# Order of weight loads and activation stores on the sync queue of a PEER decoder kernel

## The reference

```python
q = (xt @ w_q).reshape(T, 8, 2, 128)                   # queries, 8 heads, two halves
s = jnp.einsum('thpc,hpnc->thpn', q, sub_keys)
s1, i1 = lax.top_k(s[:, :, 0], 16)
s2, i2 = lax.top_k(s[:, :, 1], 16)
top_s, top_j = lax.top_k(cand, 16)                     # cand: the 16 x 16 sums of s1 and s2
expert = jnp.take_along_axis(cidx, top_j, axis=-1)     # 16 experts for each token and head
gate = jax.nn.softmax(top_s, axis=-1)
h = jax.nn.gelu(jnp.einsum('cd,chkd->chk', xc, u[ec])) # u, v: 16384 x 1024, f32
out = jnp.einsum('chk,chkd->cd', gc * h, v[ec])
```

## Time and profile before

| | us |
|---|---|
| median of 3 runs | 3217.59 (3217.42 to 3220.31) |
| the profiled execution, its own time | 3212.85 |
| its span | 3211.1 |
| PE busy in the span | 3122.8 (97%) |
| DVE busy | 2582.2 (80%) |
| ACT busy | 1630.2 (51%) |
| POOL busy | 1098.8 (34%) |

### The profile page before, as it was taken

How to read it: one execution, slowest core, us unless ns; L and a number is a source line. 1 busy time by engine, 2 the same in 40 slices (tenths; PEclk the granted TensorE clock), 3 DMA queues, 4 the chain that set the end, 5 groups by cost and what they waited for, 6 DMA issues and landing times. The chain is left out here.

```text
span 3211.1 us, 48802 instructions
## 1 busy us (share of the span) xinstructions
PE 3122.8 (97%) x17820; PEld 2787.3 (87%) x17820; DVE 2582.2 (80%) x5352; ACT 1630.2 (51%) x3075; POOL 1098.8 (34%) x658
## 2 busy tenths in 40 slices
PE   8999999999999999999999989999999999999999
PEld 7878899999998888888978868899999998888887
DVE  5686898989867888885368876898989866888885
ACT  5343249686853333334346654248686853333333
POOL 1002464646432444430000001365646432345440
PEclk9999999999999999999999999999999999999999
DMA  5113269998998999994222214259998998999994
GB/s 194 44 61 132 90 222 348 317 371 313 383 380 316 378 393 394 393 358 136 75 84 75 87 60 152 79 197 342 317 374 317 371 381 322 379 399 394 391 373 146
DMA packets 331165, 846.03 MB, mean 263 GB/s; under 512 B 27600, under 2 KB 160304, under 8 KB 323760
## 3 DMA queue, kind: packets, MB, share of 16 engines
q1 hardware_dynamic: 252592, 557.68, 48.3%
q0 software_dynamic: 78336, 285.25, 23.9%
HBM read 735.77 MB, written 107.05 MB: 262 GB/s over the span
## 5 line engine op out<-in xcount | busy, mean ns | idle before, releaser
L2545 ACT ACTIVATE peer_hi<-raw 128x1024 fp32r<-128x1024 f32 x540 | 570.9, 1057 | 706.3 <-PE p_bank L2476 623.1
L2888 DVE TENSOR_TENSOR peer_lo<-raw,peer_hi 128x1024 fp32r<-128x1024 f32 x434 | 530.6, 1223 | 303.3 <-ACT peer_hi L2545 285.2
L2358 POOL TENSOR_TENSOR peer_lo<-raw,peer_hi 128x1024 fp32r<-128x1024 f32 x106 | 272.7, 2574 | 1044.1 <-ACT peer_hi L2545 1043.7
L2376 POOL DMA_INDIRECT p_grow<-in_v_rows,p_expert x256 | 394.4, 1541 | 473.6 <-DVE p_acc L2912 381.8
L2376 POOL DMA_INDIRECT p_grow<-in_u_rows,p_expert x256 | 377.4, 1474 | 438.8 <-DVE p_hid L2903 388.7
L2476 PE MATMUL p_bank<-peer_hi,p_w_hi 128*128 128x512 f32 x1500 | 461.8, 389 | 0.0
L2476 PE MATMUL p_bank<-peer_hi,p_w_lo 128*128 128x512 f32 x1500 | 461.8, 389 | 0.0
L2476 PE MATMUL p_bank<-peer_lo,p_w_hi 128*128 128x512 f32 x1500 | 461.7, 389 | 0.0
L2402 PE MATMUL p1r_h_ps<-h_hi,peer_hi 128*128 128x368 f32 (+2 forms) x1152 | 393.7, 342 | 10.6 <-DVE peer_lo L2888 5.4
L2402 PE MATMUL p0r_h_ps<-h_hi,peer_hi 128*128 128x368 f32 (+2 forms) x1152 | 395.6, 343 | 7.7 <-DVE peer_lo L2888 5.3
L2402 PE MATMUL p0r_h_ps<-h_hi,peer_lo 128*128 128x368 f32 (+2 forms) x1152 | 389.3, 338 | 0.0
(11 more groups left out here) (481 smaller groups left out, 5615.3 us busy)
## 6 DMA issues: line engine op xcount, KB each, us to landing
raw<-in_u SPq DMA_DIRECT2D x256, 512.0 KB
raw<-in_v SPq DMA_DIRECT2D x256, 512.0 KB
p_g_sb<-gates SPq DMA_DIRECT2D x64, 768.0 KB
hiddens<-p_h_sb SPq DMA_DIRECT2D x240, 192.0 KB
p_w_raw<-hiddens SPq DMA_DIRECT2D x60, 768.0 KB
gates<-x SPq DMA_DIRECT2D x24, 1024.0 KB
raw<-in_w_b_mix SPq DMA_DIRECT2D x38, 512.0 KB, 3.5
raw<-in_w_peer_q SPq DMA_DIRECT2D x32, 512.0 KB, 4.3
```

The lines of the kernel that those rows point to most:

```text
L2358: pool.tensor_tensor(lo[:, m % NH, :], raw[:, m % NR, :], hi[:, m % NH, :].bitcast(F32), ALU.subtract).then_inc(lo_pool, 1)
L2376: pool.indirect_dma_start(out=grow[:, g % RG, :], out_offset=None, in_=table, in_offset=bass.IndirectOffsetOnAxis(ap=names[:, at:at + 1], ...
L2545: act.activation(hi[:, n % NH, :], raw[:, n % NR, :], ACT.Copy).then_inc(hi_ready, 1)
L2888: dve.tensor_tensor(lo[:, m % NH, :], raw[:, m % NR, :], hi[:, m % NH, :].bitcast(F32), ALU.subtract).then_inc(lo_dve, 1)
```

## The change

The load of block n+5 now stands ahead of the store of block n-1 in the sync list; before, it was the load of block n+4 behind that store. One load is put ahead of the loop for it. `h_sb` has four buffers instead of two. A group of gates is stored in four pieces of 512 KB, in steps s, s+1, s+2 and s+3, instead of two of 1 MB in s and s+1. To make room for the buffers, `xfew` lies in `qT` (its load moves from step 4 to step 18 and waits for the last scores) and `few_row` lies in `table`.

```diff
+    HB = 4
+    GATE_PARTS = 4
-        h_sb = st.sb("h_sb", [P, 2, SD])
+        h_sb = st.sb("h_sb", [P, HB, SD])
-            xfew = early.sb("xfew", [P, D])
+            xfew = qT[:, :, :].rearrange("p a b -> p (a b)")
-            few_row = early.sb("few_row", [P, HK])
+            few_row = table[:, BATCH * NK:BATCH * NK + HK]
             def store_g(b, part):
                 sp.wait_ge(g_moved, (b + 1) * (TB // GROUP))
-                at = slice(part * NK // 2, (part + 1) * NK // 2)
+                at = slice(part * NK // GATE_PARTS, (part + 1) * NK // GATE_PARTS)
...
             def load_few_x():
                 sp.wait_ge(few_x_stored, 16)
+                sp.wait_ge(scored, NQ)
...
+            load(NR)
             for n in range(BLOCKS + 1):
+                if n + 1 + NR < BLOCKS:
+                    load(n + 1 + NR)
                 if NQ < n <= FRONT - HELD * CH:
                     store_h(n - 1)
-                if n + NR < BLOCKS:
-                    load(n + NR)
                 if n == 2:
                     store_few_x()
-                if n == 4:
+                if n == NQ + 2:
                     load_few_x()
...
-                if n in store_at:
-                    store_g(store_at[n], 0)
-                if n - 1 in store_at:
-                    store_g(store_at[n - 1], 1)
+                for part in range(GATE_PARTS):
+                    if n - part in store_at:
+                        store_g(store_at[n - part], part)
...
-                if j >= 2:
-
-                    act.wait_ge(h_stored[j % 2], 16 * (j // 2))
+                if j >= HB:
+
+                    act.wait_ge(h_stored[j % HB], 16 * (j // HB))
...
-                    act.wait_ge(g_stored[b % 2], 32 * (b // 2))
+                    act.wait_ge(g_stored[b % 2], 16 * GATE_PARTS * (b // 2))
```

More of the change, by code:

```diff
@@ L2171, in peer_stage @@
         loaded = [st.sem(f"loaded{r}") for r in range(NR)]
-        h_stored = [st.sem(f"h_stored{r}") for r in range(2)]
+        h_stored = [st.sem(f"h_stored{r}") for r in range(HB)]
         g_stored = [st.sem(f"g_stored{r}") for r in range(2)]
@@ L2249, in store_h @@
                 sp.wait_ge(taken, n + 1)
-                sp.dma_start(h_dram[j // CH, :, j % CH, :], h_sb[:, j % 2, :]).then_inc(h_stored[j % 2], 16)
+                sp.dma_start(h_dram[j // CH, :, j % CH, :], h_sb[:, j % HB, :]).then_inc(h_stored[j % HB], 16)
             def store_g(b, part):
                 sp.wait_ge(g_moved, (b + 1) * (TB // GROUP))
-                at = slice(part * NK // 2, (part + 1) * NK // 2)
+                at = slice(part * NK // GATE_PARTS, (part + 1) * NK // GATE_PARTS)
                 sp.dma_start(g_dram[:, (b + 1) % NTD, at, :], gbuf[b % 2][:, at, :]).then_inc(g_stored[b % 2], 16)
@@ L2259, in load_hidden @@
                 at = chunk_source(c)
-                for r in range(2):
-                    sp.wait_ge(h_stored[r], 16 * (at + 1) * CH // 2)
+                for r in range(HB):
+                    sp.wait_ge(h_stored[r], 16 * (at + 1) * CH // HB)
                 sp.dma_start(w_raw[:, c % 2, :, :], h_dram[at]).then_inc(h_loaded[c % 2], 16)
@@ L2266, in load_gates @@
                     for r in range(2):
-                        sp.wait_ge(g_stored[r], 32 * (NTD // 2))
+                        sp.wait_ge(g_stored[r], 16 * GATE_PARTS * (NTD // 2))
                 else:
@@ L2281, in load_few_x @@
                 sp.wait_ge(few_x_stored, 16)
-                sp.dma_start(xfew[:, :], few_x_dram.rearrange("t q d -> (t q) d")).then_inc(few_x_loaded, 16)
+                sp.wait_ge(scored, NQ)
+                sp.dma_start(xfew, few_x_dram.rearrange("t q d -> (t q) d")).then_inc(few_x_loaded, 16)
             def store_few():
@@ L2561, in take @@
                     return
-                if j >= 2:
-                    act.wait_ge(h_stored[j % 2], 16 * (j // 2))
-                else:
-                    unit(h_sb[:, j % 2, 0:NE])
-                act.activation(h_sb[:, j % 2, NE:SD], h_ps[:, n % 2, P + NE:S], ACT.Gelu).then_inc(taken, 1)
+                if j >= HB:
+                    act.wait_ge(h_stored[j % HB], 16 * (j // HB))
+                else:
+                    unit(h_sb[:, j % HB, 0:NE])
+                act.activation(h_sb[:, j % HB, NE:SD], h_ps[:, n % 2, P + NE:S], ACT.Gelu).then_inc(taken, 1)
             def unit(to):
@@ L2898, in use_row @@
                         dve.wait_ge(few_x_loaded, 16)
-                    dve.tensor_tensor_reduce(row, row, xfew[:, :], 1.0, 0.0, ALU.mult, ALU.add,
+                    dve.tensor_tensor_reduce(row, row, xfew, 1.0, 0.0, ALU.mult, ALU.add,
                                              few_hid[:, at:at + 1]).then_inc(used, 1)
```

## The result

| | before | changed kernel |
|---|---|---|
| median, us | 3217.51 (3211.48 to 3220.31) | 3181.48 (3175.87 to 3183.22) |
| the profiled execution, its own time | 3212.85 | 3181.07 |
| span | 3211.1 | 3179.3 |

What follows compares the result with a forecast made beforehand. PE was taken to bound the kernel, with gaps caused by transfers by way of ACT. 20 us of gaps plus 4.4 of clock less 2.5 of added wait made 22 us, from 3217.6 to 3195.6 us; range 3180 to 3212.

Steps and rivals of the forecast that it cites:

- the forecast proper: Whole kernel: 12 to 32 us won, centred on 22 us or 3195.6 us; chance 0.58.
- What bounds it: PE, busy 97% of the span; only its gaps can be won, 30.7 us ended by ACT at the u blocks.
- The load's lead and the buffers: Sync queue: loads get 13 to 17 us instead of 8 to 10, activation stores 16 to 20.
- How much of the gaps goes: PE gaps ended by ACT at the u blocks: 65% goes, 20 of 30.7 us in both layers.
- Step 130: Behind the third stretch: the wait at `load_gates` grows to perhaps 10 us; only 30% of 4.05 us of gaps goes.
- Gate pieces: Gate stores: 1.25 MB a step instead of 1.77, leaving 4 us of backlog instead of 7.
- Their added wait: Gate buffer reuse: the last piece leaves two steps ahead of ACT's copy instead of four; 2.5 us lost.
- The clock: PE's lower clock level after gaps ended by ACT, 1.7 us lost in one window; 4.4 us won back.
- The gaps at the routing: PE gaps ended by DVE behind the routing, 5.4 us in one row: said to stay as they were.
- the sum 20 + 4.4 - 2.5: Whole kernel: gaps won, plus clock won, less the added gate buffer wait, gives 22 us.
- The signs: ACT's store waits near 0, u-block waits under 20 us; PE's column and copy gaps about 10; over 370 GB/s; longer `load_gates` wait.
- All of it goes: Rival: backlog never reaches ACT, so 30.7 + 6.8 = 37.5 us are won, 3180 us; chance 0.10.

Runs made afterwards that it cites:

- with DVE's low parts: The changed kernel, four gate pieces kept, with VectorE instead of GpSimd making all low parts of the third and fourth routing: 3172.25 us.
- with two halves: The changed kernel with each gate group in two stores of 1 MB instead of four pieces, load ahead and four activation buffers kept: 3172.16 us.

## Why the prediction was right, and where its sizes were not

The time lies inside the range, at its fast end; the forecast proper, 12 to 32 us won, missed it by 4 us. The way to the gain was right, and the terms for the gaps, the clock and the routing were mis-sized.

- *What bounds it.* Right: the gaps at the u blocks that ACT ended were what this change could win, and exactly those rows went. The v blocks stayed full. They were not the only thing to win: the work behind the routing, which the change leaves alone, was worth 5 us more in the experiments.
- *The load's lead and the buffers.* The mechanism was right, and the runs show more than was said: the two are one edit. Priced one by one, each is worth nothing or nearly so.
- *How much of the gaps goes.* This step was mis-sized: 65% of 30.7 us, 20 us; it was all of it. In the third stretch 65% was set between 361 and 415 GB/s, as if traffic that a stretch can't take were lost time. It is only put off: 384 GB/s were moved in the 148 us where 405 were wanted, and the rest in the 20 us behind at 406.
- *Step 130.* The wait at `load_gates` grew to 13.4 and 13.5 us, more than the 10 forecast. ACT then waited 4.8 us for a block in the first layer, and none of it reached PE; in the second it waited 6.6 us, and 1.5 reached PE, by way of DVE. The mechanism was right, and its price was set too high: 70% of the 4.05 us behind the stretch had been left standing.
- *Gate pieces.* Named as a help, on an estimate of backlog. By themselves they are one (0.31%). With the other two parts they take 9 us away again by the medians, 0.20% against before beside each, and these two intervals overlap. Their added wait had a cost of 2.5 us for PE: in the changed kernel ACT waits 2.0 us for gate stores and PE nothing; with DVE's low parts ACT waits 10.1 and PE 1.3. That price was near. What the prediction lacks is the rest of their cost, in the gaps that DVE ends: 20.3 us for 15.4 with two halves.
- *The clock.* 4.4 us were counted for windows behind gaps that ACT ended. Those were there as said, four of them with 13.7 us at the lower level, and all went. But the windows behind the routing grew from 17.1 to 30.7 us, so that the u blocks ran 30.7 us at the lower level before and after. The gaps at the routing, said to stay as they were, grew from 16.3 to 18.8 us, and two come in a row there. After the one at 2280 us in the changed kernel, and the same with two halves:

```profile
2282.00:2294.00 12.00, 11.81 (x58) 11.81 (x59) 11.40 (x21) 5.17 (x13) 5.25 (x4) 0.80 0.90 321
```

```profile
2276.00:2288.00 12.00, 12.00 (x71) 11.86 (x72) 11.93 (x21) 6.23 (x16) 5.35 (x4) 0.87 0.96 319
```

PE does 58 matmuls in 12 us where it does 71. In the first the gaps are 1.8 and 1.5 us, in the second 0.2 and 1.7. So the sum 20 + 4.4 - 2.5 should have read 30.7 for the gaps, nothing for the clock, -2.5 for the routing and -1.5 for step 130, which is 26.7. Idle time elsewhere fell by 1.0, and PE's busy time by 4.1, which was not traced; together 31.8 between the profiled spans. The medians are 36.0 apart: the 4.7 us between before's profiled execution and its median were carried over, but the changed kernel's is 0.4. The profiled execution of before had a mean granted clock of 0.993; 45 others of that kernel have 0.988 to 0.994 with a median of 0.991, and the changed kernel's four 0.992 to 0.994.
- *The signs.* Stores near 0, over 370 GB/s and the longer wait at `load_gates` came as said. ACT's wait for u blocks, 23.1 us, stayed above the 20 given, and PE's gaps at columns and copies went to 0 and not to 10.
- *The rivals.* "All of it goes" had 0.10 and 3180 us, and that is what came. Its 30.7 us of gaps are right. Its 6.8 us of clock are not, and that the total agrees is in part luck: the terms above make up for it. Its evidence, six us more for each load, was in the text; the argument against it was step 130 alone, and I didn't follow that wait on to PE.

## What to carry to other kernels

When one engine waits in turn for two transfers behind the same backlog, give both their longer lead at once and measure that: either alone only moves the wait. A stretch whose traffic exceeds the engines' rate for a while costs nothing as long as the buffers reach into the quieter stretch behind it, so weigh a burst against the lead and not against the rate. Splitting a store to smooth a burst takes from the lead of whoever reuses its source, and of whoever waits for its last piece.

## What the hardware showed that was not expected

Some VectorE instructions that start beside a GpSimd subtraction of 128x1024 f32 wait for its end (2.46 us for a TENSOR_SCALAR that takes 0.26), and others, a FIND_INDEX8 of 0.27 us, do not. Giving 18 such subtractions a layer back to VectorE, 1.22 us each, made the kernel 5 us faster, and PE's clock, which stayed up behind the short gaps that were left, made more of that than the gaps did. A store of 512 KB issued at 908.93 us in the changed kernel let its waiter go at 922.86 us, 13.9 us later, in 14 us that moved 376 GB/s:

```profile
908.93 0.49 SPq L2257 DMA_DIRECT2D gates<-p0r_gbuf  x1
922.86 0.59 SPq L2274 DMA_DIRECT2D p_g_sb<-gates  x1
```
